# Weight tiles loaded as two transfers of 512 KB in place of one of 1 MB

## The reference

```
proj = rmsnorm(h) @ w_in; kv = rmsnorm(mem) @ w_mem_kv
merged = g0*y_conv + g1*y_attn + g2*y_mem
h = h + merged @ w_o
up = causal_dwconv(rmsnorm(h) @ w_up); h = h + (silu(gt) * val) @ w_down
# second block
mod = silu(c) @ ada_w + ada_b
x = x + g1 * token_mixer(...)         # four kinds of attention
for e in range(16):                   # each token uses 2 experts of one group of 4
    he = silu(t @ w_gate[e]) * (t @ w_up[e])
    y = y + combine[:, e] * (he @ w_down[e])
```

## Time and profile before

| | |
|---|---|
| Median of 3 runs | 3093.92 us (3089.81 to 3094.66) |
| Profiled execution, its own time | 3087.46 us |
| Span of its instructions | 3085.5 us |
| TensorE busy | 96% |
| VectorE busy | 67% |
| ScalarE busy | 46% |
| Queue 1 (SyncE's loads) | 673.24 MB, 58.4% of 16 DMA engines |
| Mean granted TensorE clock | 0.98 |

### The profile page before, as it was taken

The page is one execution under the profiler, slowest core; times in us unless marked ns, Lnnn a source line. Parts: engine busy times, 40 slices in busy tenths (PEclk is TensorE's granted clock), DMA queues, the critical chain, the costliest instruction groups (busy, mean ns, idle before and its releaser), DMA issues.

```text
span 3085.5 us, 52880 instructions
## 1 busy us (share of the span) xinstructions
PE 2959.1 (96%) x21616; PEld 2808.3 (91%) x21616; DVE 2081.6 (67%) x2473; ACT 1434.3 (46%) x1546; POOL 65.7 (2%) x163
## 2 busy tenths in 40 slices
PE   5999999999999899999999989999989999999997
PEld 5899899999999899999999979988888889889887
DVE  4543447887664788888888863455664885775873
ACT  4443553344443444444444443444534564564661
POOL 0000010000000000000000000111000000000000
PEclk8999999999999999999999989999999999999998
DMA  5544545454463688888788764444314796795881
GB/s 212 179 165 166 177 154 177 177 185 169 165 221 123 262 311 323 316 319 326 314 319 327 288 187 152 146 146 149 132 44 184 295 365 229 298 345 215 329 321 66
DMA packets 113669, 692.40 MB, mean 224 GB/s; under 512 B 13888, under 2 KB 27440, under 8 KB 32368
## 3 DMA queue, kind: packets, MB, share of 16 engines
q1 hardware_dynamic: 107936, 673.24, 58.4%
q10 hardware_dynamic: 4688, 13.11, 1.5%
q0 software_dynamic: 896, 3.93, 0.4%
HBM read 679.74 MB, written 10.49 MB: 224 GB/s over the span
## 4 chain that ended last, share of the span: by engine, by line
PE 88%; DVE 5%; DMA 2%; ACT 2%; issue 1%; SPq 0%; DVEq 0%; ACTq 0%
PE psT L978 18%; PE psT L979 18%; PE psT L980 18%; PE psT L1409 2%; PE psT L1411 2%; PE psT L1410 2%; PE psT L1398 2%; PE psT L1399 2%; PE psT L1400 2%; PE psY L1075 2%; DMA raw<-tiles_dram 2%; DVE w_lo L1523 1%; PE psY L1448 1%; PE psY L1109 1%; PE psY L1449 1%
## 5 line engine op out<-in xcount | busy, mean ns | idle before, releaser
L1523 DVE TENSOR_TENSOR w_lo<-raw,w_hi 128x2048 fp32r<-128x2048 f32 x534 | 1221.4, 2290 | 565.9 <-ACT w_hi L569 562.5
L569 ACT ACTIVATE w_hi<-raw 128x2048 fp32r<-128x2048 f32 x534 | 1019.7, 1911 | 574.3 <-DMA raw<-tiles_dram 214.9
L978 PE MATMUL psT<-a_hi,w_hi 128*128 128x256 f32 x4240 | 1214.8, 287 | 50.0 <-DVE a_lo L1554 41.5
L979 PE MATMUL psT<-a_lo,w_hi 128*128 128x256 f32 x4240 | 1206.0, 284 | 0.0
L980 PE MATMUL psT<-a_hi,w_lo 128*128 128x256 f32 x4240 | 1205.6, 284 | 0.0
L978 PEld LDWEIGHTS psT<-a_hi,w_hi 128*128 128x128 f32 x4240 | 820.4, 193 | 57.3 <-issue 54.5
L979 PEld LDWEIGHTS psT<-a_lo,w_hi 128*128 128x128 f32 x4240 | 820.3, 193 | 0.3
L980 PEld LDWEIGHTS psT<-a_hi,w_lo 128*128 128x128 f32 x4240 | 819.9, 193 | 0.0
L978 PE MATMUL psT<-h_hi,w_hi 128*128 128x256 f32 (+1 forms) x800 | 230.0, 288 | 8.4 <-DVE h_lo L1778 5.8
L979 PE MATMUL psT<-h_lo,w_hi 128*128 128x256 f32 (+1 forms) x800 | 228.8, 286 | 0.0
L980 PE MATMUL psT<-h_hi,w_lo 128*128 128x256 f32 (+1 forms) x800 | 228.7, 286 | 0.0
(11 more groups left out here) (285 smaller groups left out, 3424.8 us busy)
## 6 DMA issues: line engine op xcount, KB each, us to landing
raw<-tiles_dram SPq DMA_DIRECT2D x534, 1024.0 KB, 5.6
pool<-ada_tiles_dram SPq DMA_DIRECT2D x96, 1024.0 KB, 4.8
bias_rows_dram<-pool ACTq DMA_DIRECT2D x1, 8192.0 KB, 47.7
pool<-bias_rows_dram SPq DMA_DIRECT2D x40, 128.0 KB, 4.5
pool<-bias_rows_dram SPq DMA_DIRECT2D x40, 64.0 KB, 4.6
pool<-mem_dram ACTq DMA_DIRECT2D x1, 2048.0 KB, 12.9
pool<-x_dram ACTq DMA_DIRECT2D x1, 2048.0 KB, 23.0
pool<-x_dram POOLq DMA_DIRECT2D x1, 2048.0 KB, 9.6
```

Of the source, the lines that this page charges most:

```text
L569: nc.scalar.activation(w_hi[:, t.k % SPL, :], raw[:, t.k % RAW, :], ACT.Copy).then_inc(hi_done, 1)
L978: nc.tensor.matmul(ps_out, wh, x_hi, start=first, stop=False)
L979: nc.tensor.matmul(ps_out, wh, x_lo, start=False, stop=False)
L1523: nc.vector.tensor_tensor(w_lo[:, t.k % SPL, :], raw[:, t.k % RAW, :], w_hi[:, t.k % SPL, :].bitcast(F32), ALU.subtract).then_inc(lo_done, 1)
```

## The change

Each weight tile is loaded by two transfers, columns 0 to 1023 and 1024 to 2047 of its 128 rows, issued one behind the other on SyncE's queue, both with 16 on the same semaphore. The wait for the free buffer stands before the first of them as before. ScalarE waits for 32 in place of 16 for each tile, so for both halves, and splits the whole tile at once as before. The order of tiles, buffers and all other transfers stay.

```diff
             def load_tile(t):
                 wait(sp, lo_done, (t + -RAW).count())
-                sp.dma_start(raw[:, t.k % RAW, :], tiles[t.k if t.i is None else t.i * t.n + t.k])\
-                    .then_inc(landed[t.k % RAW], 16)
+                for half in range(2):
+                    sp.dma_start(raw[:, t.k % RAW, 1024 * half:1024 * half + 1024],
+                                 tiles[t.k if t.i is None else t.i * t.n + t.k][:, 1024 * half:1024 * half + 1024])\
+                        .then_inc(landed[t.k % RAW], 16)
...
                     t = Tile(at + k)
                     wait(sp, lo_done, (t + -RAW).count())
-                    sp.dma_start(raw[:, t.k % RAW, :], tiles[group[s] * 48 + (BASE["moe"] + 12 * j + 4 * part + k)])\
-                        .then_inc(landed[t.k % RAW], 16)
+                    for half in range(2):
+                        sp.dma_start(raw[:, t.k % RAW, 1024 * half:1024 * half + 1024],
+                                     tiles[group[s] * 48 + (BASE["moe"] + 12 * j + 4 * part + k)][:, 1024 * half:1024 * half + 1024])\
+                            .then_inc(landed[t.k % RAW], 16)
...
                 wait(act, used, (t + -SPL).count())
-                act.wait_ge(landed[t.k % RAW], t.plus(16 * (t.k // RAW + 1), 16 * (t.n // RAW)))
+                act.wait_ge(landed[t.k % RAW], t.plus(32 * (t.k // RAW + 1), 32 * (t.n // RAW)))
                 nc.scalar.activation(w_hi[:, t.k % SPL, :], raw[:, t.k % RAW, :], ACT.Copy).then_inc(hi_done, 1)
```

## The result

| | before | after |
|---|---|---|
| Median | 3092.63 us (3089.81 to 3094.66) | 3120.24 us (3116.11 to 3122.51) |
| Ratio | | 1.0088, 95% interval 1.0071 to 1.0106 |
| Profiled execution, its own time | 3087.46 us | 3118.47 us |
| Span | 3085.5 us | 3116.7 us |

The change costs 28 us. The forecast was 3096.3 us with a range up to 3112 us, and 0.27 was given to slower. Lines of after stand two to four further down: split is L573, w_lo L1527, the matmuls L982 to L984, L1402 (full-width experts) and L1413 (window experts).

What follows compares the result with a forecast made beforehand. It took TensorE, busy 96% of the span, as the bound, with loads setting the pace only in places. Terms 2.9 - 1.3 + 0.5 + 0.3 = +2.4 us on 3093.9 us gave 3096.3 us, range 3088 to 3112 us.

Steps and rivals of the forecast that it cites:

- Packets in the busy queue: Weight tiles in the full load queue: 4 KB rows for 8 KB make each 0.10 us dearer, between 0 and 0.19.
- The window runs: Three runs of window experts, 120 tiles: 75 late tiles at 0.10 us less 4.6 us margin, +2.9 us (0 to +18).
- account with a margin: Ends of the window runs: 4.6 us of TensorE's lead is used up first, then dearer tiles cost one for one.
- The gap at a run's end: Sign of being right: TensorE's gap at the end of a window run is near nothing.
- DMA share stay at 0.99: Sign of being right: DMA share at 0.99 over longer parts of the window runs, GB/s a few per cent under 389.
- The feed-forward part: 1160 to 1700 us: loads are early, so no cost there; only its opening, behind ada tiles, costs +0.3 us.
- Nothing elsewhere: Gates and projections: tiles come many us ahead of TensorE, so the change costs nothing.
- The start: First loads: smaller tile rows leave the mem load more turns, so it lands earlier, -1.3 us (0 to -1.7).
- bias loads: Local attention: bias loads queue behind a tile's second issue and dearer packets, +0.5 us for one case on the chain.
- Issues: SyncE's 534 added DMA issues: hidden beside the first half's data, cost nothing; 0.37 us a tile if uncovered.
- Rival A: Halves served in series in the full queue, +0.4 us a tile: +33 us in the window runs, 3127 us; chance 0.15.
- B: Rival: all 56 bias sets, local and second block, late by 0.47 us each: +26 us, 3120 us; chance 0.05.

Runs made afterwards that it cites:

- e2_pieces: Kernel before, still one transfer a tile, but each 8 KB row lands as two 4 KB pieces in two planes: 3094.56 us, ratio 1.0016.
- e3_contig: Changed kernel with tiles stored half by half in DRAM, so each 512 KB transfer reads one contiguous stretch: 3086.93 us, ratio 0.9993 to the kernel before.
- e7_pad: Changed kernel with 256 never-read bytes behind each 8 KB row in DRAM: 3093.37 us, ratio 1.0008 to the kernel before.
- e16_ada_after: Changed kernel with the 96 ada loads issued from GpSimd's queue in place of SyncE's: 3094.07 us, ratio 1.0006 to the kernel before.
- e1_rows: Changed kernel's two transfers cut by partitions (0 to 63, 64 to 127) in place of columns, rows whole: 3472.47 us, ratio 1.1229 to the kernel before.

## Why the prediction failed

**Packets in the busy queue: the term that was mis-sized.** "I take the middle, 0.10 us" a tile, with 0.19 us as the far end. Measured: 0.23 us. The bounds came from an output store and from bias rows, and both asked only what a packet of some size costs. The runs show that this part is small: about 5 us with 4 KB pieces of whole rows (e2_pieces), nothing that can be measured with contiguous halves (e3_contig). The step that failed is that "the trace has no load of 4 KB rows" was answered by sizes alone; the address pattern, one 4 KB piece in each 8192 bytes, was never priced. It carries most of the 28 us, as e3_contig and e7_pad show. The Trainium skill (DMA: Bandwidth & Descriptors, Latency and other measured facts) has a row on DRAM row pitches at large powers of two, measured from 512 KiB on: a pitch of 4 MiB halves a copy's rate, and 4 KiB of padding cures it where 192 bytes do not. It is measured far from 8 KB, but it would have been the right rival. Here 256 bytes of padding were enough, at a pitch of 8 KB.

**The window runs.** Place and cause were right (a full queue at a pace level with TensorE's), and the size followed from the term before: +2.9 us forecast, 16.7 us measured. The far end with 0.19 us a tile gave +18, close to it by luck, as it prices another way of paying. Wrong was the account with a margin: "uses this up first and then costs time". The margins at the runs' ends stayed (2.1, 3.0 and 1.6 us); TensorE paid in the middle, some 12 us by waits for VectorE's hidden activation and some 5 us by the lower clock behind two of them. The prediction looked only at when a weight is ready, not at what else waits behind w_lo on VectorE, and had no term for the clock. The gap at a run's end "near nothing", named as a sign of being right, did not come either, nor did the DMA share stay at 0.99: it was 0.95 in 2460 to 2480 us, with 355 GB/s.

**The feed-forward part: wrong in kind.** "TensorE is busy for all 540 us while the DMA engines are at 0.82: loads are early there." Neither half of the sentence says when a load lands. 42 splits waited for loads in that stretch, 109.5 us in all, and the rows were there to be read. The forecast for everything behind the opening was nothing; it was 12.6 us, outside the sum and its range altogether. The e16_ada_after run shows the cause: the tile's issue is bound to VectorE through the ada loads ahead of it. "Nothing elsewhere" holds for gates and projections.

**The start.** Forecast -1.3 us with mem at about 12.4 us or earlier; mem landed after 11.5 us and the first w_lo 2.1 us earlier. Right, and not only in one trace: mem lands after 12.8 to 13.3 us in the five traces with whole 8 KB rows in one transfer at the start, and after 10.8 to 12.1 us in the eight with halves by columns. Though the last of it is gone by tile 64, past the bias loads (+2.2 us over tiles 0 to 64, forecast +0.5).

**Issues.** "Cost nothing" is right: 1068 issues with contiguous halves cost nothing that can be measured, and so, nearly, do 2136.

**The rivals.** Rival A (halves in series, 3127 us) and B (bias loads, 3120 us) came near the number, but neither is what happened: e3_contig keeps two transfers of 512 KB and loses nothing, so no fixed part of a transfer is paid; and in B's stages (tiles 0 to 64, 284 to 342) only 3 us went. The same run answers the rule on transfer sizes. The Trainium skill (DMA: Bandwidth & Descriptors, Rules for kernel authors) asks for at least 1 MiB a transfer for the most bandwidth; here halves of 512 KB, and quarters of 256 KB with padding, went as fast as 1 MB or within 0.3% of it, in a queue that always has the next one waiting.

## What to carry to other kernels

Cutting a load in two by columns changes the addresses as well as the sizes: rows that were contiguous become pieces at an even spacing. Store the parts contiguously, or pad the row by a few hundred bytes, and the number of transfers matters little. And "the engine is busy and the DMA share is under 1" does not say that loads have lead: read who waits for the loads, what stands ahead of them in their queue, and what stands behind them on the engine that takes them. A short wait of TensorE can also cost more than its own length, so read the granted clock behind it. A load stream that must never be late should not share a queue with loads that wait for another engine.

## What the runs showed of the hardware

- Reads of 4 KB at a spacing of 8192 bytes, lower and upper 4 KB in turn, took 187 ns a packet beside 172 ns for contiguous ones; with 256 bytes of padding 179 ns. Not all packets pay: in the changed kernel the median is still 159 ns.
- The lower 4 KB alone, at the same spacing, cost a third as much in time (10 for 28 us), and nothing in the feed-forward part.
- With weight tiles loaded into 64 partitions at a time (e1_rows) the DMA engines were full at 263 GB/s in the feed-forward part, where the ada loads still fill 128, and at 231 GB/s in 2700 to 2720 us, where the tiles are alone; loads into 128 partitions reach 389 GB/s.
- 96 loads of 1 MB issued by GpSimd in place of SyncE ran beside VectorE's work, and the kernel was 0.28% faster (landing 6.2 us, median, in the feed-forward stretch).
- Behind waits of 2.1 and 3.9 us in the window runs the granted clock over 20 us was 0.91 and 0.83 (a part of them at 1.2 GHz); behind another of 2.1 us it stayed at 1.00.
